# State space convolution: bias and last tap moved from TensorE to GpSimd and VectorE

## The chip, the cores and the metric

The kernel runs on all 8 cores of one Trainium2 chip, one batch element to a core, with the same program and no exchange between cores. The metric is the device time in microseconds of the slowest core.

## The reference, cut to what matters

Two layers of a hybrid decoder. Each layer adds to x (8 x 2048 x 1024, float32) the output projection of four mixers that share one normalised input projection, and then a SwiGLU. One of the mixers is a state space scan, whose input first goes through a causal convolution of four taps along the sequence, each of 768 channels by itself, with a bias and a silu:

```python
SSM_CONV_K = 4
SSM_CONV_DIM = SSM_D_INNER + 2 * SSM_GROUPS * SSM_D_STATE   # 768
...
def ssd_mixer(h, conv_w, conv_b, dt_bias, a_log, d_skip, norm_w):
    z, xbc, dt = jnp.split(h, [SSM_D_INNER, SSM_D_INNER + SSM_CONV_DIM], axis=-1)
    xbc = lax.conv_general_dilated(
        xbc, conv_w.T[:, None, :], window_strides=(1,), padding=[(SSM_CONV_K - 1, 0)],
        dimension_numbers=('NWC', 'WIO', 'NWC'), feature_group_count=SSM_CONV_DIM)
    xbc = jax.nn.silu(xbc + conv_b)
    xs, Bm, Cm = jnp.split(xbc, [SSM_D_INNER, SSM_D_INNER + SSM_GROUPS * SSM_D_STATE], axis=-1)
```

The other mixers are a gated MLP over chunks of 128 positions, a pooling over windows of 2 to 16 positions, and a differential attention.

## The kernel before, in words

Activations lie transposed, channels on the 128 partitions and positions along the free dimension, in slabs of 512 positions. The sequence of 2048 is worked in two halves `h` of two slabs `s` each. The outer loops are: layer `li`, half `h`, and in them `mixing(li, h)` followed by `swiglu(li, h)`.

In `mixing`, the state space part runs for each slab over six blocks `cb` of 128 channels. `b1_proj` projects a block with eight matmuls; ScalarE copies the result as bf16 into `cin[cb % 2]`, behind three carried columns that GpSimd copies in and out of `carry`. `b1_conv` then makes the convolution on TensorE: one matmul with 12 rows adds the bias (`cvb` holds it as a high and a low bf16 part, six rows each, and the moving operand is one constant column repeated 512 times), and four matmuls with the diagonal matrices `dws[:, cb, kk, :]` add the taps, each reading `cin` shifted by one position. `silu2` closes: tanh on ScalarE, reading PSUM, then one `scalar_tensor_tensor` on VectorE, whose second input is the PSUM bank. The results are scaled by two, as the tanh form of silu leaves them. After the six blocks `b2_chunk` runs the scan, four chunks of 128 positions a slab, and `ssd_norm` its norm. The attention and the output projection with the second norm follow.

`layer_params` loads each layer's parameters once, builds the 24 diagonal matrices with VectorE, and makes the two-part biases with `hilo`. The gating bias `gbs` of the first mixer is such a one too, of 8 rows.

The order of all instructions on all five queues is not that of the text. `Prog.schedule` takes the atoms (a matmul group between `begin` and `end`, or one instruction), their dependencies and a modelled duration for each, and puts them in order greedily: the earliest possible start first, ties by priority. `mixing` has a high priority (`P.bias = 2000`), `swiglu` the lowest (`P.bias = None`), so that the SwiGLU of one half fills TensorE's gaps in the mixing of the next. PSUM banks are given out by the same planner. In `mixing(0, 0)` there is nothing yet to fill with.

The calls of a slab:

```python
            for cb in range(6):
                if cb + 1 < 6:
                    b1_proj(s, cb + 1)
                b1_conv(s, cb)
            for c in range(4 * s, 4 * s + 4):
                b2_chunk(c)
```

Of the kernel before, what the change touches and what calls it, by code (L numbers as in the profile page):

```python
# [8 lines left out]
F32 = mybir.dt.float32  # L9
BF16 = mybir.dt.bfloat16  # L10
# [571 lines left out]
GELU_C = 0.7978845608028654  # L582


CP_N1W, CP_N2W, CP_CONVW, CP_DCOL, CP_SSMNW, CP_PSCALE, CP_QNW, CP_KNW, CP_SUBLN = 0, 8, 16, 40, 42, 44, 46, 47, 48
NCOLP = 49

RP_GMNW, RP_DTB, RP_ALOG, RP_LQ1, RP_LK1, RP_LQ2, RP_LK2 = 0, 256, 260, 264, 296, 328, 360
NROWP = 392

CF_U, CF_SL, CF_ALIBI, CF_INVWIN, CF_INVC16, CF_M6, CF_M4 = 0, 128, 256, 324, 326, 358, 360
NCF = 362
CB_IDENT, CB_U, CB_NEG, CB_BD32, CB_BD64, CB_HEAD, CB_CB, CB_SEL = 0, 128, 256, 384, 512, 640, 644, 650
NCB = 682


def make_consts():
    cf = np.zeros((128, NCF), np.float32)
    cb = np.zeros((128, NCB), np.float32)
    j = np.arange(128)[:, None]  # L600
    l = np.arange(128)[None, :]
    cf[:, CF_U:CF_U + 128] = (j <= l)
    cf[:, CF_SL:CF_SL + 128] = (j > l)
    for h in range(4):
        for e in range(17):
            cf[:, CF_ALIBI + h * 17 + e] = SLOPES[h] * (np.arange(128) - 128.0 * e)
# [6 lines left out]
    cf[0:6, CF_M6] = 1.0
    cf[6:12, CF_M6 + 1] = 1.0
    cf[0:4, CF_M4] = 1.0
    cf[4:8, CF_M4 + 1] = 1.0
    cb[:, CB_IDENT:CB_IDENT + 128] = np.eye(128)
    cb[:, CB_U:CB_U + 128] = (j <= l)
    cb[:, CB_NEG:CB_NEG + 128] = np.where(j <= l, 0.0, NEGV)
    cb[:, CB_BD32:CB_BD32 + 128] = (j // 32 == l // 32)  # L620
    cb[:, CB_BD64:CB_BD64 + 128] = (j // 64 == l // 64)
    for p in range(8):
        cb[p, CB_HEAD + p % 4] = 1.0
    for p in range(12):
        cb[p, CB_CB + p % 6] = 1.0
    for p in range(96):
        cb[p, CB_SEL + p % 32] = 1.0
    return cf, cb
# [31 lines left out]
def build(nlayers=2):  # L660
# [10 lines left out]
    wd_d = din("ffn_w_down", [2, DFF, D])  # L671
    wsT_d = din("gm_wsT", [2, 4, 128, 128])
    gbs_d = din("gm_bs", [2, 4, 128])
    cvb_d = din("ssm_conv_b", [2, 6, 128])
    poolw_d = din("pool_w", [2, 4, 64, 64])
    colp_d = din("colp", [2, 128, NCOLP])
    rowp_d = din("rowp", [2, 1, NROWP])
# [35 lines left out]
    colp = sb("colp", [128, NCOLP], F32)  # L713
    rowp = sb("rowp", [128, NROWP], F32)
    small = sb("small", [128, 32], F32)
    cvb = sb("cvb", [12, 128], BF16)
    gbs = sb("gbs", [8, 128], BF16)
    wsTm = sb("wsTm", [128, 4, 128], BF16)
    wdt = sb("wdt", [128, 8, 4], BF16)
    dtp = sb("dtp", [128, 6, 32], F32)  # L720
    atm3 = tp[:, 1024:1024 + 384].bitcast(F32)
    R3 = sb("R3", [128, 128], BF16)
    hist = sb("hist", [128, 2, 16], F32)
    carry = sb("carry", [128, 6, 4], BF16)
    wbd = sb("wbd", [128, 2, 128], BF16)
    dws = sb("dws", [128, 6, 4, 128], BF16)
    Sst = sb("Sst", [128, 256], F32)
    Sbf = sb("Sbf", [128, 256], BF16)
    Psum.ap = es.enter_context(nc.psum_tensor(PSUM_NAME, [128, 8, 512], F32))
# [2 lines left out]
    Ub = cB[:, CB_U:CB_U + 128]  # L732
    NEGb = cB[:, CB_NEG:CB_NEG + 128]
    bd32b = cB[:, CB_BD32:CB_BD32 + 128]
    bd64b = cB[:, CB_BD64:CB_BD64 + 128]
    Uf = cF[:, CF_U:CF_U + 128]
    SLf = cF[:, CF_SL:CF_SL + 128]
    neghalf = small[:, 31:32]
# [59 lines left out]
    def layer_params(li, pbuf, pbase):  # L798

        lam_init = 0.8 - 0.6 * math.exp(-0.3 * li)  # L800
        load_w(wsTm[:], wsT_d[li].rearrange("h s t -> s h t"), 'wsT')
        for cc in range(2):
            P.memset('pool', wbd[:, cc, :], 0.0)
            for gg in range(2):
                load_w(wbd[gg * 64:(gg + 1) * 64, cc, gg * 64:(gg + 1) * 64], poolw_d[li][2 * cc + gg], 'wbd')
        tb = Bump(pbuf, pbase, pbase + 6 * KB)
        cf2 = tb.alloc([128], F32)[0:12]
        ch2 = tb.alloc([128], BF16)[0:12]
        for r in range(2):
            P.dma('sp', cf2[6 * r:6 * r + 6], cvb_d[li], 'cvb', wrs=[cf2[6 * r:6 * r + 6]], kb=6)  # L810
        hilo(cvb[:], cf2, ch2, cF[0:12, CF_M6:CF_M6 + 1], cF[0:12, CF_M6 + 1:CF_M6 + 2])
        gf2 = tb.alloc([128], F32)[0:8]
        gh2 = tb.alloc([128], BF16)[0:8]
        lt = tb.alloc([32], F32)
        for r in range(2):
            P.dma('sp', gf2[4 * r:4 * r + 4], gbs_d[li], 'gbs', wrs=[gf2[4 * r:4 * r + 4]], kb=2)
        P.ts('dve', gf2, gf2, 0.5, None, op0=ALU.mult)
        hilo(gbs[:], gf2, gh2, cF[0:8, CF_M4:CF_M4 + 1], cF[0:8, CF_M4 + 1:CF_M4 + 2])
        P.stt(wsTm[:], wsTm[:], 0.5, Ub.unsqueeze(1).to_broadcast([128, 4, 128]), ALU.mult, ALU.mult)
        for k, (ra, rb) in enumerate(((RP_LQ1, RP_LK1), (RP_LQ2, RP_LK2))):  # L820
            P.tt('dve', lt, rowp[:, ra:ra + 32], rowp[:, rb:rb + 32], ALU.mult)
            P.rsum(lam2[:, k:k + 1], lt)
        P.act(lam2, lam2, AF.Exp)
        P.tt('dve', neglam, lam2[:, 1:2], lam2[:, 0:1], ALU.subtract)
        P.ts('dve', neglam, neglam, -lam_init, None, op0=ALU.add)
        P.ts('dve', qnws, colp[:, CP_QNW:CP_QNW + 1], SM_SCALE, None, op0=ALU.mult)
        P.ts('dve', subc, colp[:, CP_SUBLN:CP_SUBLN + 1], 1.0 - lam_init, None, op0=ALU.mult)
        P.ts('dve', dcol, colp[:, CP_DCOL:CP_DCOL + 2], 0.5, None, op0=ALU.mult)
        P.act(Ab, rowp[:, RP_ALOG:RP_ALOG + 4], AF.Exp)
        P.ts('dve', Ab, Ab, -1.0, None, op0=ALU.mult)  # L830
        for cb in range(6):
            for kk in range(4):
                cw = CP_CONVW + cb * 4 + kk
                P.ts('dve', dws[:, cb, kk, :], identb, colp[:, cw:cw + 1], None, op0=ALU.mult)
        P.memset('dve', carry[:], 0.0)
        P.memset('dve', hist[:], 0.0)
        P.memset('dve', Sst[:], 0.0)
        P.memset('dve', Sbf[:], 0.0)

    def mixing(li, h):  # L840
# [87 lines left out]
        for t in range(8):  # L928
# [124 lines left out]
        def b2_chunk(c):
            s, cl = c // 4, slice((c % 4) * 128, (c % 4) * 128 + 128)
# [282 lines left out]
def host_pack(inputs):  # L1337
# [4 lines left out]
    for l in range(2):  # L1342
        colp[l, :, CP_N1W:CP_N1W + 8] = f('norm1_w')[l].reshape(8, 128).T
        colp[l, :, CP_N2W:CP_N2W + 8] = f('norm2_w')[l].reshape(8, 128).T
        colp[l, :, CP_CONVW:CP_CONVW + 24] = f('ssm_conv_w')[l].reshape(6, 128, 4).transpose(1, 0, 2).reshape(128, 24)
        for hc in range(2):
            colp[l, :, CP_DCOL + hc] = f('ssm_d')[l][2 * hc + p // 64]
        colp[l, :, CP_SSMNW:CP_SSMNW + 2] = f('ssm_norm_w')[l].reshape(2, 128).T
        colp[l, :, CP_PSCALE:CP_PSCALE + 2] = f('pool_scale')[l].reshape(2, 128).T
        colp[l, :, CP_QNW] = f('da_q_norm_w')[l][p % 32]  # L1350
        colp[l, :, CP_KNW] = f('da_k_norm_w')[l][p % 32]
        colp[l, :, CP_SUBLN] = f('da_subln_w')[l][p % 64]
        rowp[l, 0, RP_GMNW:RP_GMNW + 256] = f('gm_norm_w')[l].reshape(256)
# [41 lines left out]
```

How the kernel before makes its waits and increments, by code:

```python
        def run(engname, e):  # L472
            for waits, thunk, tok in plan[engname]:
                alone = list(waits) if thunk is None else list(waits[:-1])
                for k in range(0, len(alone), 2):
                    w_ins = e.wait_ge(semh[alone[k][0]], alone[k][1])
                    if k + 1 < len(alone):
                        w_ins._wait_ge(semh[alone[k + 1][0]], alone[k + 1][1])
                if thunk is None:
                    continue
                ins = thunk(e)
                if waits:
                    s, v = waits[-1]
                    ins._wait_ge(semh[s], v)
                ins.then_inc(semh[tok[0]], 16 if tok[0].startswith('d_') else 1)
```

## Time and profile before

| | |
|---|---|
| median of 3 runs | 1833.38 us (1832.42 to 1893.77) |
| the profiled execution | 1833.44 us |
| its span on the slowest core | 1831.9 us (cores 1822.4 to 1831.9) |
| TensorE busy | 1723.5 us, 94% |
| VectorE busy | 1033.6 us, 56% |
| ScalarE busy | 802.4 us, 44% |
| GpSimd busy | 505.4 us, 28% |
| mean granted TensorE clock, core 0 | 0.966 of full |

Busy time is the union of an engine's instructions over the span of the slowest core. Matmuls overlap, so the duration of one is longer than the distance between two starts.

### The profile page before, as it was taken

To read this page: it belongs to the slowest core of one execution; us is meant where nothing else is said; L and a number is where in the kernel's file an instruction comes from. 1 tells how busy PE (TensorE), PEld (TensorE's weight loads), DVE (VectorE), ACT (ScalarE), POOL (GpSimd) and SP (SyncE) were. 2 spreads that over 40 slices of the span, in tenths; PEclk is the share of its full clock that TensorE was granted. 3 is DMA by queue.
4 is the path that set the end of the run, shared out by engine and by line. 5 is a ranking of instruction groups with operands and counts; after the bars stand their busy time and mean duration, and the time that the engine had idled before them with its cause. 6 is when DMAs were issued, how large, how long until landed. Compare 5 with 4: busy or idle time off the path is not lost.

```text
span 1831.9 us, 25845 instructions; the slowest of 8 cores (1822.4 to 1831.9 us)
## 1 busy us (share of the span) xinstructions
PE 1723.5 (94%) x10492; PEld 793.1 (43%) x10492; DVE 1033.6 (56%) x1947; ACT 802.4 (44%) x1218; POOL 505.4 (28%) x659
## 2 busy tenths in 40 slices
PE   3998789999999999999999988999999999999998
PEld 0444334444444444544444443444444444444443
DVE  2766547767533458668655456666664333655555
ACT  1477633446576723213455553225466674211110
POOL 4345444633121121024332232033431111100000
PEclk9997589999999999999999999999999999999999
DMA  9303944324630249752145246930517202684433
GB/s 181 43 24 67 199 94 56 52 29 60 124 64 7 45 83 150 148 75 43 30 63 97 42 89 123 164 51 1 92 24 138 42 6 58 110 162 74 70 46 104
DMA packets 123464, 143.38 MB, mean 78 GB/s; under 512 B 9128, under 2 KB 91600, under 8 KB 123344
## 3 DMA queue, kind: packets, MB, share of 16 engines
q0 software_dynamic: 100912, 99.11, 36.7%
q1 hardware_dynamic: 22432, 42.61, 7.1%
q8 instruction: 83, 1.36, 0.3%
q14 instruction: 37, 0.30, 0.1%
HBM read 224.03 MB, written 16.78 MB: 131 GB/s over the span
## 4 chain that ended last, share of the span: by engine, by line
PE 85%; DVE 6%; ACT 5%; DMA 2%; POOL 2%; issue 0%; SPq 0%; DVEq 0%; ACTq 0%
PE ps L513 84%; DVE s_hT L551 2%; DMA s_x<-xT 1%; ACT s_x L532 1%; PE ps L517 1%; ACT s_tmp L532 1%; ACT s_pt L532 1%; DVE s_x L541 1%; ACT L532 1%; POOL s_mix L541 1%; POOL s_x L541 0%; DVE s_ring L551 0%; DVE s_ring L541 0%; DMA s_x<-xspill 0%; DVE s_sg L551 0%
## 5 line engine op out<-in xcount | busy, mean ns | idle before, releaser
L513 PE MATMUL ps<-s_hT,s_ring 128*128 128x512 bf16 x2816 | 665.3, 383 | 5.4 <-DVE s_hT L551 4.0
L541 DVE TENSOR_TENSOR s_x<-s_x,ps 128x512 f32<-128x512 f32 (+2 forms) x496 | 317.7, 671 | 195.4 <-PE ps L513 184.4
L513 PEld LDWEIGHTS ps<-s_hT,s_ring 128*128 128x128 bf16 x2816 | 265.4, 98 | 308.8 <-issue 20.6
L513 PE MATMUL ps<-s_act,s_ring 128*128 128x512 bf16 x1408 | 343.6, 385 | 15.6 <-DVE s_sg L551 9.7
L532 ACT ACTIVATE s_sg<-ps 128x512 f32<-128x512 f32 x176 | 104.7, 597 | 420.3 <-PE ps L513 419.7
L551 DVE SCALAR_TENSOR_TENSOR s_sg<-s_sg,ps 128x512 f32<-128x512 f32 x176 | 119.8, 685 | 241.4 <-ACT s_sg L532 135.9
L541 POOL TENSOR_TENSOR s_x<-s_x 128x512 bf16<-128x512 f32 (+2 forms) x116 | 111.9, 965 | 332.4 <-DVE s_x L541 218.4
L513 PEld LDWEIGHTS ps<-s_act,s_ring 128*128 128x128 bf16 x1408 | 131.1, 99 | 164.9 <-issue 12.7
L513 PE MATMUL ps<-s_hT,s_x 128*128 128x512 bf16 x768 | 181.8, 387 | 1.3 <-DVE s_hT L551 1.0
L551 DVE SCALAR_TENSOR_TENSOR s_act<-s_sg,ps 128x512 bf16<-128x512 f32 x176 | 119.7, 685 | 72.0 <-PE ps L513 70.5
L513 PE MATMUL ps<-s_x,s_k 32*128 32x512 bf16 (+3 forms) x668 | 115.7, 344 | 8.8 <-ACT s_act L532 1.8
L532 ACT ACTIVATE s_pt<-ps,s_cF 128x1024 bf16<-128x1024 f32 (+3 forms) x109 | 97.1, 890 | 47.2 <-PE ps L513 46.9
L513 PEld LDWEIGHTS ps<-s_hT,s_x 128*128 128x128 bf16 x768 | 75.4, 99 | 94.6 <-DVE s_hT L551 5.3
L216 POOL DMA_DIRECT2D s_ring<-ffn_w_down x24 | 18.9, 788 | 318.1 <-PE ps L513 317.3
L532 ACT ACTIVATE s_tmp<-ps,s_cF 128x1024 bf16<-128x1024 f32 (+3 forms) x92 | 84.8, 923 | 45.1 <-PE ps L513 44.3
L532 ACT ACTIVATE s_x<-ps,s_cF 128x1024 bf16<-128x1024 f32 (+3 forms) x92 | 82.5, 897 | 39.2 <-PE ps L513 38.0
L513 PE MATMUL ps<-s_mix,s_hT 128*128 128x260 bf16 (+1 forms) x512 | 91.5, 327 | 2.9 <-DVE s_x L541 2.9
L541 POOL TENSOR_TENSOR s_mix<-s_x 128x512 bf16<-128x512 f32 x48 | 54.3, 1137 | 137.3 <-PE ps L513 120.9
L532 ACT ACTIVATE s_x<-ps 128x512 f32<-128x512 f32 x84 | 49.8, 596 | 86.5 <-PE ps L513 62.5
L532 ACT ACT_TABLE_LOAD x64 | 82.1, 1283 | 2.8 <-PEq L661 1.1
L513 PEld LDWEIGHTS ps<-s_x,s_k 32*128 32x128 bf16 x668 | 31.5, 91 | 104.0 <-issue 49.6
L551 DVE SCALAR_TENSOR_TENSOR s_hT<-s_x,s_colp,s_tmp 128x512 bf16<-128x512 f32 x64 | 45.2, 768 | 45.1 <-ACT s_tmp L532 45.1
(196 smaller groups left out, 2028.1 us busy)
## 6 DMA issues: line engine op xcount, KB each, us to landing
s_ring<-ffn_w_gate POOLq DMA_DIRECT2D x20, 1024.0 KB, 13.3
s_ring<-ffn_w_up POOLq DMA_DIRECT2D x20, 1024.0 KB, 11.8
s_ring<-ffn_w_down POOLq DMA_DIRECT2D x20, 1024.0 KB, 10.1
s_x<-w_in POOLq DMA_DIRECT2D x12, 1024.0 KB, 24.6
s_x<-xT SPq DMA_DIRECT2D x16, 512.0 KB, 5.9
s_x<-xT SPq DMA_DIRECT2D x8, 1024.0 KB, 11.7
xspill<-s_x SPq DMA_DIRECT2D x8, 1024.0 KB, 13.9
s_x<-xspill SPq DMA_DIRECT2D x8, 1024.0 KB, 8.4
```

What stands on the lines that cost most here:

```text
L216: self.add(Op(queue, lambda e: e.dma_start(out=out, in_=in_), list(rds), list(wrs), dur, None, 'd_' + key, kb))
L513: self.op('pe', lambda e: e.matmul(real(out), lhsT, rhs, start=start, stop=stop), [lhsT, rhs], [out], d if dur is None else dur)
L517: self.op('pe', lambda e: e.transpose(real(out), in_, ident), [in_, ident], [out], 0.06)
L532: self.op('act', lambda e: e.activation(out, real(in_), func, **kw), rd, [out], d, self.TAB.get(func))
L541: self.op(eng, lambda e: e.tensor_tensor(out, real(in0), real(in1), op), [in0, in1], [out], d)
L551: self.op('dve', lambda e: e.scalar_tensor_tensor(out, real(in0), scalar, real(in1), op0, op1), [in0, scalar, in1], [out], 0.06 + self.vdu ...
```

## The change

The bias and the last tap are computed together by one GpSimd `tensor_scalar` per block: `u = ci[:, 3:515] * w3 + bias`, from bf16 to float32, with both scalars taken from per-partition columns of `colp`. TensorE does only the taps 0 to 2 and no bias. VectorE adds the PSUM bank to `u` in place, and `silu2` reads `u` from SBUF, with ScalarE and with VectorE. `uu` holds two such buffers. The constants for the bias (`cvb`, its selector columns and masks, its DMAs and its `hilo`) go, as do six of the 24 diagonal matrices of a layer. `gbs` moves from partitions 0 to 7 of a buffer of its own to partitions 96 to 103 of `R3`, and unused constants go.

```diff
+    uu = sb("uu", [128, 2, 512], F32)
...
-    cvb = sb("cvb", [12, 128], BF16)
-    gbs = sb("gbs", [8, 128], BF16)
...
+    gbs = R3[96:104, :]
...
-    dws = sb("dws", [128, 6, 4, 128], BF16)
+    dws = sb("dws", [128, 6, 3, 128], BF16)
...
-        cf2 = tb.alloc([128], F32)[0:12]
-        ch2 = tb.alloc([128], BF16)[0:12]
-        for r in range(2):
-            P.dma('sp', cf2[6 * r:6 * r + 6], cvb_d[li], 'cvb', wrs=[cf2[6 * r:6 * r + 6]], kb=6)
-        hilo(cvb[:], cf2, ch2, cF[0:12, CF_M6:CF_M6 + 1], cF[0:12, CF_M6 + 1:CF_M6 + 2])
-        gf2 = tb.alloc([128], F32)[0:8]
-        gh2 = tb.alloc([128], BF16)[0:8]
+        gf2 = tb.alloc([128], F32)[96:104]
+        gh2 = tb.alloc([128], BF16)[96:104]
...
         for cb in range(6):
-            for kk in range(4):
+            for kk in range(3):
                 cw = CP_CONVW + cb * 4 + kk
                 P.ts('dve', dws[:, cb, kk, :], identb, colp[:, cw:cw + 1], None, op0=ALU.mult)
...
-            P.mm(pg[:, 0:256], gbs[:], cB[0:8, CB_HEAD:CB_HEAD + 4].unsqueeze(2).to_broadcast([8, 4, 64]), start=True, stop=False)
+            P.mm(pg[:, 0:256], gbs, cB[96:104, CB_HEAD:CB_HEAD + 4].unsqueeze(2).to_broadcast([8, 4, 64]), start=True, stop=False)
...
+        us = [uu[:, k, :] for k in range(2)]
...
         def b1_conv(s, cb):
             ci = cin[cb % 2]
             dst = slabs[s % len(slabs)][1 + cb // 2][:, cb % 2, :]
+            u = us[cb % len(us)]
+            cw = CP_CONVW + cb * 4 + 3
+            P.ts('pool', u, ci[:, 3:515], colp[:, cw:cw + 1], colp[:, CP_CONVB + cb:CP_CONVB + cb + 1], op0=ALU.mult, op1=ALU.add)
             b = P.tile(m1)
             P.begin()
             P.guards = [dst]
-            P.mm(b, cvb[:], cB[0:12, CB_CB + cb:CB_CB + cb + 1].to_broadcast([12, 512]), start=True, stop=False)
-            for kk in range(4):
-                P.mm(b, dws[:, cb, kk, :], ci[:, kk:kk + 512], start=False, stop=(kk == 3))
+            for kk in range(3):
+                P.mm(b, dws[:, cb, kk, :], ci[:, kk:kk + 512], start=(kk == 0), stop=(kk == 2))
             P.end()
-            silu2(dst, b)
+            P.tt('dve', u, u, b, ALU.add)
+            silu2(dst, u)
```

## Rows read from the trace of the kernel before

**Rows 1.** The page's busy time by engine: us, share of the span, instructions.

```profile
PE 1723.5 (94%) x10492; PEld 793.1 (43%) x10492; DVE 1033.6 (56%) x1947; ACT 802.4 (44%) x1218; POOL 505.4 (28%) x659
```

**Rows 2.** The page's 40 slices: TensorE busy and granted clock, in tenths.

```profile
PE   3998789999999999999999988999999999999998
...
PEclk9997589999999999999999999999999999999999
```

**Rows 3.** Windows on core 0: length, busy time by engine, granted clock, DMA share, GB/s.

```profile
60.00:110.00 50.00, 47.45 (x254) 23.26 (x253) 31.04 (x88) 25.81 (x45) 20.19 (x36) 0.97 0.01 2
110.00:170.00 60.00, 54.84 (x417) 26.13 (x416) 40.19 (x88) 43.08 (x74) 34.31 (x48) 0.83 0.22 53
170.00:230.00 60.00, 44.10 (x383) 22.91 (x383) 34.22 (x72) 40.56 (x67) 29.39 (x31) 0.63 0.91 170
...
340.00:450.00 110.00, 109.90 (x658) 51.47 (x655) 72.40 (x167) 55.97 (x105) 47.52 (x79) 1.00 0.25 37
...
830.00:960.00 130.00, 129.99 (x756) 60.05 (x754) 89.53 (x186) 59.61 (x112) 54.70 (x89) 1.00 0.25 40
...
1230.00:1330.00 100.00, 98.82 (x587) 46.60 (x587) 66.64 (x148) 46.57 (x89) 42.66 (x73) 1.00 0.27 43
```

**Rows 4.** Timeline of TensorE around two convolutions, 402 to 415 us: start, length, what.

```profile
401.96 7.07 PE L513 MATMUL ps<-s_hT,s_x 128*128 128x512 bf16 x32
...
408.96 0.39 PE L513 MATMUL ps<-s_cB,s_cvb 12*128 12x512 bf16 x1
409.28 1.04 PE L513 MATMUL ps<-s_wx,s_dws 128*128 128x512 bf16 x4
...
410.25 0.38 PE L513 MATMUL ps<-s_cB,s_cvb 12*128 12x512 bf16 x1
...
410.57 1.04 PE L513 MATMUL ps<-s_wx,s_dws 128*128 128x512 bf16 x4
...
411.44 3.62 PE L513 MATMUL ps<-s_hT,s_x 128*128 128x512 bf16 x16
```

**Rows 5.** Groups by shape, whole span: busy us, mean ns; idle before and releasers.

```profile
L541 DVE TENSOR_TENSOR s_x<-s_x,ps 128x512 f32<-128x512 f32 x448 | 292.3, 684 | 181.4 <-PE ps L513 173.0 <-DMA s_x<-xspill 6.3
...
L541 POOL TENSOR_TENSOR s_x<-s_x 128x512 bf16<-128x512 f32 x56 | 64.4, 1151 | 67.3 <-DVE s_x L558 37.5 <-PE ps L513 15.3 <-DVE s_x L551 10.4
...
L532 ACT ACTIVATE s_x<-s_x 128x512 f32<-128x512 f32 x68 | 42.5, 628 | 5.4 <-DVE s_x L551 5.2
...
L551 DVE SCALAR_TENSOR_TENSOR s_hT<-s_x,s_colp,s_mix 128x512 bf16<-128x512 f32 x64 | 44.7, 768 | 9.0 <-ACT s_mix L532 9.0
...
L551 DVE SCALAR_TENSOR_TENSOR s_x<-s_wx,ps 128x512 bf16<-128x512 f32 x48 | 32.1, 685 | 51.1 <-PE ps L513 36.6 <-ACT s_wx L532 14.3
...
L532 ACT ACTIVATE s_wx<-ps 128x512 f32<-128x512 f32 x48 | 27.6, 596 | 30.7 <-PE ps L513 19.5 <-DVE s_x L551 11.2
...
L541 POOL TENSOR_TENSOR s_ring<-s_ring,s_x 128x512 bf16<-128x512 f32 x8 | 10.6, 1321 | 4.9 <-ACT s_ring L532 4.9
L558 POOL COPY s_wx<-s_carry 128x3 bf16<-128x3 bf16 x36 | 7.7, 217 | 22.9 <-PE ps L513 22.9
...
L547 DVE TENSOR_SCALAR s_dws<-s_cB,s_colp 128x128 bf16<-128x128 bf16 x48 | 8.5, 254 | 0.8 <-DMA s_colp<-colp 0.7
```

**Rows 6.** The chain that ended last, first half: start, us, what, instructions.

```profile
71.40 10.78 PE ps L513 x51
...
103.14 9.99 PE ps L513 x46
...
128.06 12.11 PE ps L513 x75
...
164.09 1.37 PE ps L513 x5
```

**Rows 7.** The same chain where one half hands over to the next.

```profile
256.23 7.03 POOL s_mix L541 x7
...
1135.42 7.36 DVE s_hT L551 x12
```

More of the change, by code:

```diff
@@ L582 @@
 GELU_C = 0.7978845608028654
-CP_N1W, CP_N2W, CP_CONVW, CP_DCOL, CP_SSMNW, CP_PSCALE, CP_QNW, CP_KNW, CP_SUBLN = 0, 8, 16, 40, 42, 44, 46, 47, 48
-NCOLP = 49
+CP_N1W, CP_N2W, CP_CONVW, CP_DCOL, CP_SSMNW, CP_PSCALE, CP_QNW, CP_KNW, CP_SUBLN, CP_CONVB = 0, 8, 16, 40, 42, 44, 46, 47, 48, 49
+NCOLP = 55
 RP_GMNW, RP_DTB, RP_ALOG, RP_LQ1, RP_LK1, RP_LQ2, RP_LK2 = 0, 256, 260, 264, 296, 328, 360
 NROWP = 392
[L591 to L594, printed above, removed]
+CF_U, CF_SL, CF_ALIBI, CF_INVWIN, CF_INVC16, CF_M4 = 0, 128, 256, 324, 326, 358
+NCF = 360
+CB_IDENT, CB_U, CB_NEG, CB_BD32, CB_HEAD, CB_SEL = 0, 128, 256, 384, 512, 516
+NCB = 548
 def make_consts():
@@ L612, in make_consts @@
                 cf[p, CF_INVC16 + c * 16 + t] = 1.0 / min(t + 1, win)
[L613 to L616, printed above, removed]
+    cf[96:100, CF_M4] = 1.0
+    cf[100:104, CF_M4 + 1] = 1.0
     cb[:, CB_IDENT:CB_IDENT + 128] = np.eye(128)
@@ L620, in make_consts @@
     cb[:, CB_BD32:CB_BD32 + 128] = (j // 32 == l // 32)
-    cb[:, CB_BD64:CB_BD64 + 128] = (j // 64 == l // 64)
     for p in range(8):
-        cb[p, CB_HEAD + p % 4] = 1.0
-    for p in range(12):
-        cb[p, CB_CB + p % 6] = 1.0
+        cb[96 + p, CB_HEAD + p % 4] = 1.0
     for p in range(96):
@@ L673, in build @@
     gbs_d = din("gm_bs", [2, 4, 128])
-    cvb_d = din("ssm_conv_b", [2, 6, 128])
     poolw_d = din("pool_w", [2, 4, 64, 64])
@@ L715, in build @@
     small = sb("small", [128, 32], F32)
-    cvb = sb("cvb", [12, 128], BF16)
-    gbs = sb("gbs", [8, 128], BF16)
     wsTm = sb("wsTm", [128, 4, 128], BF16)
-    wdt = sb("wdt", [128, 8, 4], BF16)
     dtp = sb("dtp", [128, 6, 32], F32)
@@ L734, in build @@
     bd32b = cB[:, CB_BD32:CB_BD32 + 128]
-    bd64b = cB[:, CB_BD64:CB_BD64 + 128]
     Uf = cF[:, CF_U:CF_U + 128]
@@ L817, in layer_params @@
         P.ts('dve', gf2, gf2, 0.5, None, op0=ALU.mult)
-        hilo(gbs[:], gf2, gh2, cF[0:8, CF_M4:CF_M4 + 1], cF[0:8, CF_M4 + 1:CF_M4 + 2])
+        hilo(gbs, gf2, gh2, cF[96:104, CF_M4:CF_M4 + 1], cF[96:104, CF_M4 + 1:CF_M4 + 2])
         P.stt(wsTm[:], wsTm[:], 0.5, Ub.unsqueeze(1).to_broadcast([128, 4, 128]), ALU.mult, ALU.mult)
@@ L1345, in host_pack @@
         colp[l, :, CP_CONVW:CP_CONVW + 24] = f('ssm_conv_w')[l].reshape(6, 128, 4).transpose(1, 0, 2).reshape(128, 24)
+        colp[l, :, CP_CONVB:CP_CONVB + 6] = f('ssm_conv_b')[l].reshape(6, 128).T
         for hc in range(2):
@@ L1368, in host_pack @@
         "gm_bs": np.ascontiguousarray(f('gm_bs')),
-        "ssm_conv_b": np.ascontiguousarray(f('ssm_conv_b').reshape(2, 6, 128)),
         "pool_w": np.ascontiguousarray(f('pool_w')),
```

## The prediction

> **What bounds the kernel now.** I read the page's busy line first: TensorE is busy 1723.5 of 1831.9 us, 94%, against 56% for VectorE, 44% for ScalarE and 28% for GpSimd [rows 1]. The 40 slices of 45.8 us then say where the missing 6% is: the first slice (input and first norm, 3 tenths), slices 4 to 6 (8, 7 and 8 tenths), and specks later; the granted clock is 7, 5 and 8 tenths in slices 4 to 6 and about full after [rows 2]. The reader should see two kernels in one: the first half of layer 0 (to about 230 us), with no SwiGLU to fill in, and the rest, where it fills.
>
> The windows make it plain [rows 3]. The three later stretches with the convolutions, 340 to 450, 830 to 960 and 1230 to 1330 us, hold 48 tap matmuls each (12 convolutions), and TensorE is busy 109.9 of 110, 130.0 of 130 and 98.8 of 100 us at granted clock 1.00. There time is TensorE work and nothing else. The first half holds the other 12 convolutions: TensorE is busy 102.3 of 110 us between 60 and 170, then only 44 of 60, with the clock at 0.83 and 0.63.
>
> **What a convolution costs TensorE.** The timeline of a stretch without a stall gives start-to-start times [rows 4]. An ordinary 512-column matmul takes (3.62 - 0.38) / 15 = 0.216 us. The one of 12 rows starts 408.96 - (401.96 + 7.07 - 0.38) = 0.31 us after its predecessor, and the first tap starts 0.32 us after it; four taps to the next projection are 411.44 - 410.57 = 0.87, four ordinary steps. So the bias matmul is dearer than its 512 columns: 0.10 us extra on entering it and 0.10 on leaving it. Before: 0.10 + 0.32 + 4 x 0.216 = 1.28 us. After: 3 x 0.216 = 0.65. Saved: 0.63 us for each of the 48 convolutions (6 blocks x 2 slabs x 2 halves x 2 layers), 30.2 us of TensorE work.
>
> The Trainium skill, "TensorE: Matmul & The Clock Gate", section "Why this matters for your kernels", says that a matmul of few rows takes the same time as one of 128. By that the saving would be 96 x 0.216 = 20.7 us. The trace disagrees at the seams. "TensorEngine Tiling (Array Packing)", section "Key Properties", says that a change of tiling mode drains the array; the two seams of 0.10 us fit that. I go by the rows.
>
> **The covered convolutions.** 36 x 0.63 = 22.7 us leave stretches in which TensorE has 1.3 us of idle time in 340 [rows 3]. Nothing has to be made up elsewhere: the SwiGLU atoms fill in whatever waits. I count all 22.7.
>
> **What is added.** VectorE: 48 additions, one input in PSUM, at 0.684 us (the same form stands in the profile), and the closing scalar_tensor_tensor reads both tensors from SBUF: 0.768 us in the nearest row against 0.685 now [rows 5]. That is 48 x (0.684 + 0.083) = 36.8 us; 12 of the 48 diagonal builds go (12 x 0.254 = 3.0) and eight small operations for the bias. In 340 to 450 VectorE goes from 72.4 by 12 x 0.77 = 9.2 to 82 of 110 us: hidden. Cost nothing there; without TensorE as cover it would be 9.2 us a half. ScalarE: tanh from SBUF instead of PSUM, 0.628 against 0.596, 1.5 us in all, hidden.
>
> GpSimd: 48 tensor_scalar with two per-partition scalars, 128x512, bf16 to f32. No such form is in the trace. From below: the 3-column copy, 0.217 us. From above: the slowest tensor_tensor form of this size, 1.321. The commonest is 1.151; I take 1.1, since width and conversion are the same and one input fewer can only help [rows 5]. In 340 to 450 GpSimd goes from 47.5 to 61 of 110 us; even at 1.321 to 63. The Trainium skill, "GPSIMD Engine Reference", section "Engine selection", would put elementwise work on VectorE: GpSimd about twice slower with two inputs, roughly level with one. No run here shows the one-input case; by it the instruction would be near 0.7 us and my total about 2 us lower.
>
> **The waits it adds.** The addition waits for three taps and for GpSimd. Behind it on VectorE stand evictions of SwiGLU and of the state space chunks, and behind those TensorE's PSUM banks. The tensor_scalar waits for ScalarE's copy of the projection, and behind it on GpSimd stand the carry copies, for which the next convolution's matmuls wait, and the issues of ring weights. One convolution's time from copy to silu: before 1.18 us of matmuls; after 1.1 + 0.68, and 0.08 + 0.03 in the silu, with one more handover: longer by about 0.8 to 0.9 us. In the covered halves two `cin` buffers and the fill hide that: a block's eleven matmuls take 2.4 us, above GpSimd's 1.1 and VectorE's 1.5.
>
> **The first half.** There 12 x 0.63 = 7.5 us of TensorE work goes, in a stretch (60 to 170 us) where TensorE is 93% busy. Against it stands the longer way. The chain runs through TensorE blocks that hold convolutions at 71, 103, 128 and 164 us, with a fifth pair inside the first [rows 6]: five times 0.9 = 4.5 us. I book 7.5 - 4.5 = 3.0 us of gain, with bounds of -5 (all twelve pay the 0.9, 10.8 us, and VectorE's 9.2 us press on it, little of the saving arrives) and +7.5 (no latency shows). From 170 to 205 the chain is VectorE and GpSimd work of the chunks, which the change doesn't touch. The other edits (dropped constants, four small SP transfers, the gating bias now in rows 96 to 103 of `R3`, still one narrow matmul) I put at zero: the transfers ran beside the input norm.
>
> **The sum.** 22.7 + 3.0 = 25.7 us. The profiled execution took 1833.44 us with a span of 1831.9, and the median is 1833.38, so they are the same time: 1833.4 - 25.7 = 1807.7, forecast 1808, 1.4% faster. What is late next is still TensorE: its work falls to about 1693 us. A measurement of this kernel tells about 2% from no change, so I expect "within 2%".
>
> **Rivals.**
> A. The seams stay: they belong to the start of an accumulation group and not to the 12 rows. For: both are at a group's start. Against: projections start groups without one, 411.44 being an example. Then 20.7 - 5.2 = 15.5 us covered, and 5.2 - 4.5 = 0.7: 1833.4 - 16.2 = 1817. Chance 0.10.
> B. The planner's order. `schedule` is greedy and rebuilds the order of 25,000 instructions; TensorE's idle time (1831.9 - 1723.5 = 108 us, almost all outside the covered convolutions) isn't fixed. The hand-overs are the fragile places: 7.0 us of GpSimd squares at 256 us and 7.4 us of VectorE at 1135 us stand alone on the chain [rows 7]. If such a place opens twice more, 14 us go: 1808 + 14 = 1822. Chance 0.18.
> C. Slower: GpSimd paces the first half. If each tensor_scalar queues behind another operation of its size (1.151), the way per convolution grows by 2.0 us, 12 x 2.0 = 24, less the 7.5 saved: 16.5 us. TensorE then idles more between 60 and 130, where the clock was 0.97, and falls to 1.2 GHz, as it did to 0.63 in the stretch with 44 of 60 us busy: 60 us of work at 0.63 in place of 0.97 cost 60 x (0.97/0.63 - 1) = 32 us. 1833.4 - 22.7 + 16.5 + 32 = 1859. It decides for slower once the first half loses over 22.7 us. Against: GpSimd is busy 20 of 50 and 34 of 60 us there. Chance 0.04.
> D. All 30.2 us arrive, no latency shows, and the first half keeps the clock better. A mean of 0.63 over 60 us [rows 3] is some 44 us at 1.2 GHz and the rest at 2.4; if 16 of the 44 us went at 2.4, their work would take 8: 1833.4 - 30.2 - 8 = 1795. Chance 0.13. The one-input GpSimd would push this way.
>
> **How the numbers follow.** Forecast (1801 to 1816 by its own bounds) 0.55, A 0.10, B 0.18, C 0.04, D 0.13. Low end: between forecast and D, 1797, leaving 0.09 below. High end: B with 7 us more, 1829, leaving 0.07 above. Faster by over 2% (under 1796.7): most of D, 0.09. Slower by over 2% (over 1870): the far part of C, 0.01. The rest, 0.90, is the same.
>
> **What the profile after would show.** No matmul of 12 rows; 144 tap matmuls; TensorE's start-to-start 0.22 us into and through the taps; three stretches with convolutions still 99% busy and 7.5 us shorter each; VectorE about 1067 us, GpSimd about 558. A tensor_scalar of 1.1 us. Wrong would be: TensorE idle before the addition's release in covered stretches, convolution pairs in the first half spread further apart, or work gone but idle grown by as much (B).

## The result, and the profile after

The changed kernel takes 1803.9 us (1801.9 to 1804.0) against 1833.4: a ratio of 0.9838, 95% interval 0.981 to 0.9867. Timed again beside its own variants it gave 0.9837 (0.9822 to 0.9853). That is 29.5 us or 1.6% less, and clear of the noise; I had forecast 25.7 us, and that a measurement could hardly tell it from no change. Runs in which one die was disturbed, in either kernel, are left out of every ratio here.

The page of the profiled execution (1801.94 us, its slowest core 1800.4), against [rows 1, 2]:

```profile
span 1800.4 us, 25725 instructions; the slowest of 8 cores (1788.1 to 1800.4 us)
## 1 busy us (share of the span) xinstructions
PE 1693.7 (94%) x10396; PEld 789.6 (44%) x10396; DVE 1059.5 (59%) x1975; ACT 813.9 (45%) x1226; POOL 542.5 (30%) x707
...
PE   3996888999999999999999999999999999999998
...
PEclk9996698999999999999999999999999999999999
```

TensorE lost 29.8 us of busy time and 96 matmuls; what is left over, 1800.4 - 1693.7 = 106.7 us of idle, was 1831.9 - 1723.5 = 108.4. So the first reading is simple: the work went, the idle time stayed about what it was. GpSimd gained 37 us where I had 53, VectorE 26 where I had 34.

Windows, answering to [rows 3] (the first three at the same times, the others around the later convolutions, which start earlier now; core 1):

```profile
60.00:110.00 50.00, 46.30 (x256) 23.13 (x254) 36.62 (x88) 28.68 (x50) 27.59 (x44) 0.97 0.06 18
110.00:170.00 60.00, 48.95 (x367) 25.33 (x365) 53.90 (x121) 44.03 (x79) 50.36 (x64) 0.83 0.35 78
170.00:230.00 60.00, 49.20 (x444) 25.68 (x444) 23.81 (x49) 41.27 (x61) 20.09 (x21) 0.63 0.79 137
...
350.00:430.00 80.00, 77.59 (x442) 37.29 (x441) 57.71 (x125) 39.37 (x72) 39.75 (x70) 0.98 0.21 32
845.00:920.00 75.00, 75.00 (x438) 35.69 (x438) 56.14 (x109) 35.77 (x67) 37.33 (x65) 1.00 0.11 15
1210.00:1285.00 75.00, 75.00 (x437) 35.59 (x436) 53.95 (x108) 37.43 (x68) 36.44 (x66) 1.00 0.27 43
```

Two of the three later stretches are full to the last digit. The first of them is not: it has 2.4 us of idle in 80, and in the wider window of [rows 3], 340 to 450 us, TensorE is busy 106.6 of 110 us (105.6 on core 0), where it was 109.9. Only 0.3 us of it is a wait for the new addition. The rest waits for results of ScalarE and VectorE that the change does not touch:

```profile
PE ps L513 <- ACT s_mix L556: 0.9, 1, 0.9
PE ps L513 <- ACT s_mix L532: 0.8, 1, 0.8
PE ps L513 <- DVE s_sg L551: 0.7, 1, 0.7
...
PE ps L513 <- DVE s_uu L541: 0.3, 1, 0.3
```

The first half looks different from before: between 110 and 170 us VectorE is busy 53.9 of 60 (40.2 before) and GpSimd 50.4 (34.3), and after 170 both are light. The planner has written another order: the last tap matmul of the first half starts at 147.9 us, before at 165.1.

TensorE around a convolution, against [rows 4]:

```profile
407.66 3.63 PE L513 MATMUL ps<-s_hT,s_x 128*128 128x512 bf16 x16 [0.35 <-DVE s_uu L541]
411.12 0.81 PE L513 MATMUL ps<-s_wx,s_dws 128*128 128x512 bf16 x3
411.77 3.62 PE L513 MATMUL ps<-s_hT,s_x 128*128 128x512 bf16 x16
```

Last projection matmul at 407.66 + 3.63 - 0.38 = 410.91, first tap at 411.12, next projection at 411.77: 0.21 us in, 0.65 for the three taps. The seams are gone. The first line also shows the new wait, 0.35 us for VectorE's addition: it is there, and rare (over the whole span TensorE waits for the buffer `uu` four times, 3.2 us in all).

What the new instructions cost, by the tile `uu` (duration ns: least, median, most):

```profile
L541 DVE TENSOR_TENSOR s_uu<-s_uu,ps x48: 670/686/689, 74.5 to 1285.8; 128x512 f32<-128x512 f32 x48
L547 POOL TENSOR_SCALAR s_uu<-s_wx,s_colp x36: 757/768/1307, 360.5 to 1284.6; 128x512 f32<-128x512 bf16 x36
...
L551 DVE SCALAR_TENSOR_TENSOR s_x<-s_wx,s_uu x36: 681/685/1528, 373.1 to 1289.9; 128x512 bf16<-128x512 f32 x36
```

GpSimd's instruction takes 0.77 us in the median, not 1.1; single ones take up to 1.67, and the mean is 0.84. The closing operation with both tensors in SBUF has the median that it had with one in PSUM, 0.685; single ones take up to 1.53 us, the means of the two groups are 0.73 and 0.82, and nothing here shows what lengthens them.

### The profile page after: what moved, and what is told of

Read it like the earlier page. It is cut to its first block, busy times and chain, and to the rows that moved or that the text cites. A ratio compares the mean times of both kernels' runs of the same rounds, so it can differ in the third digit from the quotient of the medians.

```text
span 1800.4 us, 25725 instructions; the slowest of 8 cores (1788.1 to 1800.4 us)
## 1 busy us (share of the span) xinstructions
PE 1693.7 (94%) x10396; PEld 789.6 (44%) x10396; DVE 1059.5 (59%) x1975; ACT 813.9 (45%) x1226; POOL 542.5 (30%) x707
## 4 chain that ended last, share of the span: by engine, by line
PE 87%; DVE 5%; ACT 4%; DMA 2%; POOL 1%; issue 1%; SPq 0%; DVEq 0%; ACTq 0%; POOLq 0%
PE ps L513 86%; DVE s_hT L551 2%; DMA s_x<-xT 2%; ACT s_x L532 1%; PE ps L517 1%; DVE s_x L541 1%; ACT s_tmp L532 1%; DVE s_ring L541 1%; ACT L532 1%; ACT s_pt L532 0%; DVE s_x L551 0%; DVE s_sg L551 0%; ACT s_act L532 0%; POOL s_x L541 0%; SPq L216 0%
## 5 line engine op out<-in xcount | busy, mean ns | idle before, releaser
L216 POOL DMA_DIRECT2D s_ring<-ffn_w_down x24 | 18.9, 787 | 300.9 <-PE ps L513 295.8
L513 PE MATMUL ps<-s_mix,s_hT 128*128 128x260 bf16 (+1 forms) x512 | 96.7, 337 | 4.1 <-DVE s_hT L551 2.7
L541 POOL TENSOR_TENSOR s_mix<-s_x 128x512 bf16<-128x512 f32 x48 | 50.4, 1052 | 105.4 <-PE ps L513 88.9
L532 ACT ACTIVATE s_x<-ps 128x512 f32<-128x512 f32 x72 | 42.5, 596 | 84.7 <-PE ps L513 51.6
L513 PEld LDWEIGHTS ps<-s_mix,s_hT 128*128 128x128 bf16 x512 | 49.6, 100 | 44.5 <-DVE s_hT L551 4.9
## 6 DMA issues: line engine op xcount, KB each, us to landing
s_ring<-ffn_w_up POOLq DMA_DIRECT2D x20, 1024.0 KB, 11.1
s_x<-xT SPq DMA_DIRECT2D x8, 1024.0 KB, 10.4
```

The lines of the kernel that those rows point to most:

```text
L216: self.add(Op(queue, lambda e: e.dma_start(out=out, in_=in_), list(rds), list(wrs), dur, None, 'd_' + key, kb))
L513: self.op('pe', lambda e: e.matmul(real(out), lhsT, rhs, start=start, stop=stop), [lhsT, rhs], [out], d if dur is None else dur)
L532: self.op('act', lambda e: e.activation(out, real(in_), func, **kw), rd, [out], d, self.TAB.get(func))
L541: self.op(eng, lambda e: e.tensor_tensor(out, real(in0), real(in1), op), [in0, in1], [out], d)
```

## The experiments

Each ratio is against the kernel before, on the same chip; 0.001 is 1.8 us. Many of them hold the order of instructions: the planner is told that an added operation lasts nothing, or that a removed one is still there, so that the queues differ by that operation alone. Where that was not done, the instruction and the order changed together, and with the order the PSUM banks that the planner gives out.

**The bias matmul over 128 rows.**

```diff
-            P.mm(b, cvb[:], cB[0:12, ...].to_broadcast([12, 512]), start=True, stop=False)
+            P.mm(b, cvb[:], cB[:, ...].to_broadcast([128, 512]), start=True, stop=False)
```

> The kernel before, with its bias matmul widened from 12 to 128 rows (rows 12 to 127 are zeros), so the same 512 columns and the same result, only the row count differs. My theory (the 0.10 us seams into and out of the matmul belong to its 12 rows): every convolution loses 0.20 us of TensorE time, 48 x 0.20 = 9.6 us, start-to-start 0.22 us through the whole convolution, TensorE busy about 1714 us, time about 1824, ratio 0.995. Rival A (the seams belong to the start of an accumulation group): start-to-start stays 0.31 and 0.32 us, time unchanged at 1833. A rival by the new order of the planner doesn't apply: the modelled durations are the same, so the order is.

Ratio 0.9926 (0.9909 to 0.9942), 13.6 us less (10.6 to 16.7). The order was the same on all five engines; VectorE has two more instructions, which set the rows to zero. TensorE's timeline:

```profile
407.34 0.38 PE L513 MATMUL ps<-s_cB,s_cvb 128*128 128x512 bf16 x1
407.56 1.03 PE L513 MATMUL ps<-s_wx,s_dws 128*128 128x512 bf16 x4
408.42 0.38 PE L513 MATMUL ps<-s_cB,s_cvb 128*128 128x512 bf16 x1
408.64 1.03 PE L513 MATMUL ps<-s_wx,s_dws 128*128 128x512 bf16 x4
```

0.22 us out of the bias matmul and (408.42 - 407.56) / 4 = 0.215 into it, where [rows 4] have 0.32 and 0.31. The seams belong to the 12 rows; rival A falls. More rows of zeros make this kernel faster. The 4 us beyond the 9.6 are not the seams' work. The mean granted clock of the cores was 0.9715 in these executions against 0.9686 in the kernel before, 0.003 of the span; my estimate from that is 5 us less time lost to the lower clock. What raised the clock is not shown.

**The bias matmul left out.**

```diff
-            P.mm(b, cvb[:], cB[0:12, ...].to_broadcast([12, 512]), start=True, stop=False)
```

> The kernel before without the bias matmul: the bias is left out, four taps stay on TensorE, nothing is added elsewhere. Theory of the seams: 48 x (0.63 - 0.216) = 19.9 us of TensorE time go, time about 1813, ratio 0.989. Rule that few rows cost what 128 do: 48 x 0.216 = 10.4 us, time about 1823. If the order rebuilt by the planner matters more than either, the time falls outside 1808 to 1828.

Ratio 0.9861 (0.9847 to 0.9876), 25.5 us less, more than either theory's number. The planner's order differed here, so this mixes the 19.9 us with an order and decides nothing between them.

**A fourth tap back on TensorE.**

```diff
-            for kk in range(3):
-                P.mm(b, dws[:, cb, kk, :], ci[:, kk:kk + 512], start=(kk == 0), stop=(kk == 2))
+            for kk in range(4):
+                P.mm(b, dws[:, cb, kk % 3, :], ci[:, kk:kk + 512], start=(kk == 0), stop=(kk == 3))
```

> The changed kernel with a fourth tap matmul put back on TensorE beside the GpSimd instruction (it uses the first tap's weights again, so the fourth tap is counted twice, once wrongly). It prices one 128-row matmul of 512 columns per convolution with all else kept. Theory (TensorE work is time in every stretch, the first half too): 48 x 0.216 = 10.4 us more than the changed kernel's 1804, so 1814, ratio 0.9895. Rival (in the first half other engines set the pace): 36 x 0.216 = 7.8 us, 1812, and the first half's end does not move.

Ratio 0.9813 (0.9799 to 0.9828): more TensorE work and 4 us faster than the changed kernel. A miss for both theories, though the intervals of the two kernels just touch (0.9822 is the low end of the changed one). The planner's order was the suspect, so I held the order:

```diff
+                     ..., dur=0.0 if kk == 3 else None)
```

> The changed kernel with the fourth tap matmul put back beside the GpSimd instruction (first tap's weights again, so that tap is counted wrongly), and with the changed kernel's order held: the planner counts the extra matmul as zero. Theory (the earlier run without the extra time was the planner's new order, which saved what the matmuls cost): 48 x 0.216 = 10.4 us over the changed kernel, about 1813, TensorE idle as in the changed kernel. Rival (a tap is free beside the GpSimd path): 1801 to 1805.

Ratio 0.9856 (0.984 to 0.9872). The same instructions as the run before in another order: 0.0043 or 7.9 us apart, with intervals that do not touch. That is rival B at work, and it can help as well as hurt. But a tap now seemed to cost 3 us, not 10.4, so it was run again beside the changed kernel.

> The changed kernel once more, timed beside its fixed-order variants. 0.9838 again if the first ratio was right, 1802 to 1804 us; the other three are read against this one.

0.9837 (0.9822 to 0.9853).

> The fourth tap matmul put back in the changed kernel's order (first tap's weights again), repeated. Theory (TensorE work is time everywhere): 10.4 us over the changed kernel of the same chip. Rival (8 us or less, the later halves only): 7.8 us. If it is under 4 us, TensorE work is not all of the time.

0.9851 (0.9836 to 0.9867), 2.6 us more than the changed kernel. The spans by core tell part of why. The changed kernel (first profile), then this one:

```profile
core 0: 1788.6 us, clock 0.974
core 1: 1800.4 us, clock 0.965
core 2: 1789.9 us, clock 0.973
core 3: 1799.9 us, clock 0.963
core 4: 1799.5 us, clock 0.967
core 5: 1789.7 us, clock 0.972
core 6: 1792.3 us, clock 0.970
core 7: 1788.1 us, clock 0.971
```

```profile
core 0: 1806.0 us, clock 0.972
core 1: 1800.8 us, clock 0.971
core 2: 1801.0 us, clock 0.971
core 3: 1804.6 us, clock 0.971
core 4: 1806.7 us, clock 0.969
...
core 6: 1800.2 us, clock 0.973
```

With the extra tap every core has about the same clock and ends within 7 us. In this execution the changed kernel falls into two sets: five cores at 1788 to 1792 us, three at 1800; their mean clocks are 0.970 to 0.974 and 0.963 to 0.967. In its other executions the cores lie anywhere between 1788 and 1806 us. The metric takes the slowest. Between single cores of like clock (0.971 and 0.970 against 0.971) the tap costs 1800.8 - 1788.1 to 1792.3, 9 to 13 us, around the 10.4. Windows of the changed kernel on core 0, then core 1, show where the sets part:

```profile
320.00:360.00 40.00, 35.80 (x208) 18.45 (x211) 33.52 (x79) 17.17 (x33) 27.10 (x43) 1.00 0.17 28
530.00:550.00 20.00, 18.70 (x182) 9.02 (x184) 8.01 (x13) 16.60 (x21) 0.73 (x1) 1.00 0.01 2
625.00:655.00 30.00, 28.76 (x251) 13.38 (x255) 13.55 (x24) 19.37 (x22) 4.72 (x5) 1.00 0.11 36
```

```profile
320.00:360.00 40.00, 36.34 (x196) 18.75 (x195) 30.30 (x68) 16.11 (x32) 19.56 (x29) 0.91 0.28 45
530.00:550.00 20.00, 18.95 (x191) 9.03 (x189) 4.74 (x9) 15.86 (x18) 4.43 (x4) 0.91 0.00 1
625.00:655.00 30.00, 28.47 (x252) 12.29 (x252) 9.19 (x16) 22.20 (x23) 1.47 (x2) 0.89 0.08 10
```

Core 1 is granted 1.2 GHz for part of three stretches in which core 0 keeps 2.4, though TensorE is 90 to 96% busy in them on both. With the extra tap, core 1 keeps 1.00 at 530 and at 625.

But the slowest core is not the whole of it. On the mean of the eight cores, over all executions on that chip, the tap costs 1801.7 - 1796.3 = 5.4 us, not 10.4. The next table splits the mean span of one profile of each kernel. "Idle" is TensorE's idle time. "Slowed" is my estimate of the time lost to the lower clock: busy time x (1 - granted clock), summed over windows of 20 us. What remains is TensorE's work at full speed. Work and slowed time are good to about 3 us: the same matmuls come out as 1640.9, 1642.6 and 1643.7 us of work in three kernels.

| kernel, mean of 8 cores, us | span | work | idle to 280 us | slowed to 280 us | idle after | slowed after |
|---|---|---|---|---|---|---|
| before | 1826.9 | 1670.6 | 65.2 | 25.9 | 47.1 | 18.1 |
| changed (`after_again`) | 1797.3 | 1640.9 | 65.9 | 26.5 | 45.1 | 18.9 |
| fourth tap, held order (`a_tap_fixed2`) | 1803.1 | 1651.3 | 65.2 | 24.9 | 46.0 | 15.7 |
| fourth tap, free order (`a_tap_back`) | 1795.9 | 1651.9 | 68.5 | 32.8 | 35.7 | 7.0 |
| GpSimd twice, held order (`a_ts_fixed2`) | 1795.6 | 1643.7 | 66.7 | 24.0 | 48.6 | 12.6 |
| bare saving, old order (`b_3taps_fixed2`) | 1801.2 | 1642.6 | 67.3 | 27.4 | 48.1 | 15.8 |

The tap adds 1651.3 - 1640.9 = 10.4 us of work, the idle time stays (111.2 against 111.0), and 4.8 us less go to the lower clock (2.8 in the profiles of the first pair). So a matmul's work arrives in full as work, and the clock gives part of it back, on the mean core too. Against the held order, the free order of the same matmuls has 11 us more idle and slowed time up to 280 us, and 19 us less after.

**GpSimd's instruction twice**, free order and then held order.

```diff
             P.ts('pool', u, ci[:, 3:515], colp[:, cw:cw + 1], ...)
+            P.ts('pool', u, ci[:, 3:515], colp[:, cw:cw + 1], ...)
```

> The changed kernel with its GpSimd instruction issued twice per convolution (same inputs, same output), which makes the side path 0.77 us longer before VectorE's addition. Theory (the side path is hidden everywhere): time unchanged within 4 us of 1804, GpSimd busy up by 37 us. Rival (the prediction's step: each convolution of the first half pays its longer way): 5 to 12 times 0.77, 4 to 9 us more, and the first half ends that much later. Rival C (GpSimd paces): more than 15 us.

Ratio 0.9872 (0.9856 to 0.9889), 6 us more than the changed kernel. By itself it would have confirmed the wrong theory (the side path is felt).

> The changed kernel with the GpSimd instruction issued twice, order held: the planner counts the second as zero. Theory (hidden; the 8 us of the earlier run were the new order): within 3 us of the changed kernel's 1804. Rival (the side path ends last in the first half): 4 to 9 us more, and TensorE idle before the first SwiGLU up by as much.

Ratio 0.9825 (0.9811 to 0.9839).

> GpSimd's instruction twice, in the changed kernel's order, repeated. Theory (side path hidden): within 2 us of the changed kernel. Rival (first half pays): 4 to 9 us more.

Ratio 0.9834 (0.9816 to 0.9852), against 0.9837 of the changed kernel on that chip. GpSimd is busy 579.0 us in place of 542.5, its results come 0.77 us later, and the time does not show it. In the table TensorE's idle time up to 280 us is 66.7 us against 65.9, where twelve waits of 0.77 us would have made it 9.2 us more. So the side path is hidden in the first half. Later there are 3.5 us more of idle, and 6.3 us less of slowed time go with them. The 6 us were the order that a longer modelled duration called for: same instructions, 0.9872 against 0.9825.

**The bare saving in the old order.**

```diff
-            P.mm(b, cvb[:], cB[0:12, ...].to_broadcast([12, 512]), start=True, stop=False)
-            for kk in range(4):
-                P.mm(b, dws[:, cb, kk, :], ci[:, kk:kk + 512], start=False, stop=(kk == 3))
+            for kk in range(3):
+                P.mm(b, dws[:, cb, kk, :], ci[:, kk:kk + 512], start=(kk == 0), stop=(kk == 2), dur=...)
```

> The kernel before with neither the bias matmul nor the last tap (both are left out and nothing takes their place), and its order of instructions held on every engine: the planner is told the old duration and the old dependencies. So this is the TensorE saving of the change alone, 48 x 0.63 = 30.2 us, in the old order. Theory (TensorE's work is the time, in the first half too): 1833.4 - 30.2 = 1803, ratio 0.984, the same as the changed kernel. Rival (in the first half others set the pace): 22.7 to 25 us, time 1809 to 1811, ratio 0.987. If it is faster than the changed kernel by more than 5 us, the added work and waits cost that.

Ratio 0.9854 (0.984 to 0.9868).

> The kernel before without bias matmul and last tap (both left out), in the old order, repeated. If the added work and waits cost nothing and the new order is worth nothing, it equals the changed kernel within 2 us. If the new order is the better one, it is 3 to 6 us slower; if the additions cost, it is faster.

Ratio 0.9869 (0.9851 to 0.9886). So 24 to 27 us come from TensorE's 30.2 us of work alone. That is no matter of the slowest core: on the mean of the eight cores it is 25.6 us on this chip and 26.8 on the one of the first ratio. In the table 2.1 us more idle and 1.5 us more slowed time than before stand against it up to 280 us, so in the first half some 2 to 4 of its 7.5 us seem not to arrive. The changed kernel, with all its additions, is faster than this by 0.0032 or 6 us on the same chip (by 3 us from the first ratios). The two intervals touch, but the mean of the eight cores settles that there is a difference: 1795.1 to 1797.3 us in the executions of the changed kernel, 1801.2 to 1801.8 in those of the bare saving, 5.2 us. In the table the difference is idle time, 111.0 us against 115.4, and added work doesn't take idle time away. The dropped constants could a little, and were not tested apart; up to 110 us TensorE is idle 35.2 us in the bare saving and 34.9 in the changed kernel, so not at the start of layer 0. What is left is the new order. TensorE's first matmul of SwiGLU moves with it, on core 7 of before, of the bare saving and of the changed kernel:

```profile
L513 PE MATMUL ps<-s_hT,s_ring x2816: 376/379/634, 269.3 to 1817.2; 128*128 128x512 bf16 x188
```

```profile
L513 PE MATMUL ps<-s_hT,s_ring x2816: 376/379/634, 264.7 to 1789.4; 128*128 128x512 bf16 x188
```

```profile
L513 PE MATMUL ps<-s_hT,s_ring x2816: 377/379/634, 255.4 to 1778.6; 128*128 128x512 bf16 x188
```

The saving alone moves that start by 4.6 us, the new order by another 9.3 (2.9 to 4.1 and 7.8 to 8.2 on the mean of the cores). But it doesn't tell how much is won: the free order of `a_tap_back` has this start at 271.6 us on the mean core, the changed kernel at 257.5, and ends no later. Of the 4.4 us less of idle time only 1.4 lie before 280 us, and 3.0 after.

**The planner told 0.77 us.**

```diff
-                self.vdur(eng, width(out)))
+                0.19 + width(out) * 0.00113 if eng == 'pool' else self.vdur(eng, width(out)))
```

> The changed kernel, same instructions, but the planner is told 0.77 us for GpSimd's tensor_scalar of 512 columns in place of 1.175. Nothing but the order changes. It measures what the order alone is worth: theory: TensorE busy unchanged within 3 us, idle time moves by up to 8 us to either side, time 1796 to 1812. Rival (order is worth nothing): within 2 us of 1804. A correct duration need not give the better order.

Ratio 0.9851 (0.9832 to 0.987), 2.4 us above the changed kernel: inside the uncertainty. The true duration gave no better order.

**The tensor_scalar on VectorE.**

```diff
-            P.ts('pool', u, ...)
+            P.ts('dve', u, ...)
```

> The changed kernel with its tensor_scalar on VectorE in place of GpSimd; everything else the same. It says whether the choice of GpSimd matters. TensorE work unchanged. On VectorE the instruction (one input, SBUF) should take 0.3 to 0.6 us, 48 x 0.5 = 24 us at most. Theory (hidden in the three later halves, felt in the first, where VectorE is 54 of 60 us busy between 110 and 170): 2 to 6 us over the changed kernel, 1806 to 1810. Rival (VectorE has room everywhere): 1804, or less, since one handover between engines goes.

Ratio 0.9883 (0.9868 to 0.9897), 8 us more than the changed kernel. It takes 0.54 us there and ends a handover, and still it loses: the windows of its slowest core have 41.8 of 60 us of TensorE between 110 and 170, at a clock of 0.76, and 0.53 in the next 60 us. This kernel ran in an order of its own, and an order was worth 8 us above. So that GpSimd is the better place because it is the idle engine is likely from the windows, and not shown.

**Toward a faster kernel.** Two edits, each alone and together: one more tap off TensorE, on VectorE, and the gating bias over 128 rows.

```diff
-            for kk in range(3):
+            for kk in range(2):
...
+            P.stt(u, ci[:, 2:514], colp[:, cw - 1:cw], u, ALU.mult, ALU.add)
             P.tt('dve', u, u, b, ALU.add)
```

> The changed kernel with one more tap taken off TensorE: VectorE adds tap 2 to u by one scalar_tensor_tensor of 512 columns before it adds the PSUM bank, TensorE keeps taps 0 and 1. Theory (VectorE hidden while it is under 90% busy where TensorE is full): 48 x 0.216 = 10.4 us less TensorE work against about 48 x 0.75 = 36 us more VectorE, time about 1794, ratio 0.978. Rival (VectorE, 54 of 60 us busy between 110 and 170 in the changed kernel, becomes the pace of the first half): 12 x 0.75 = 9 us lost there, so 1800 to 1803, the same as the changed kernel, with TensorE idle up by about 8.

Ratio 0.9841 (0.9828 to 0.9854): 10.4 us of TensorE work went and nothing came of it. The first half of that kernel, the same windows as above:

```profile
110.00:170.00 60.00, 42.61 (x296) 21.60 (x294) 54.63 (x122) 43.43 (x81) 39.87 (x50) 0.85 0.40 80
170.00:230.00 60.00, 51.10 (x463) 28.43 (x464) 25.57 (x54) 43.17 (x60) 33.85 (x37) 0.50 0.49 97
```

VectorE 54.6 of 60 us, TensorE down to 42.6, then 1.2 GHz for the whole of the next 60 us. TensorE's waits for VectorE's additions into `ring` between 110 and 170 us (us in total, times, longest), in this kernel and in the changed one:

```profile
PE ps L513 <- DVE s_ring L541: 7.1, 4, 4.4
```

```profile
PE ps L513 <- DVE s_ring L541: 1.5, 2, 1.0
```

Of TensorE's 17.4 us of idle there 11.8 end with a result of VectorE; in the changed kernel it is 3.4 of 11.1. So VectorE sets the pace here, in this kernel's own order; with the order held it was not tried.

```diff
-            P.mm(pg[:, 0:256], gbs, cB[96:104, ...].to_broadcast([8, 4, 64]), start=True, stop=False)
+            P.mm(pg[:, 0:256], R3[:], cB[:, ...].to_broadcast([128, 4, 64]), start=True, stop=False)
```

> The changed kernel with the gating bias matmul (8 rows, 256 columns, 32 of them) widened to 128 rows: the whole of R3 as weights against a constant that is zero outside rows 96 to 103. Same result. The seam theory, on another matmul: start-to-start from it to the next falls from 0.21 to 0.11 us and the step into it by 0.10, 32 x 0.20 = 6.4 us less TensorE work, time 1797 to 1799, ratio 0.980, less or more by up to 6 us since the planner's order changes with one new dependency. Rival (seams only hurt 512-column matmuls): TensorE busy unchanged, time 1804.

The seam went, as with the other bias. The changed kernel, then this one:

```profile
344.83 2.75 PE L513 MATMUL ps<-s_act,s_ring 128*128 128x512 bf16 x12
347.51 0.28 PE L513 MATMUL ps<-s_cB,s_R 8*128 8x256 bf16 x1
347.72 0.29 PE L513 MATMUL ps<-s_x,s_wsTm 128*128 128x64 bf16 x4
```

```profile
340.62 4.05 PE L513 MATMUL ps<-s_hT,s_ring 128*128 128x512 bf16 x18
344.50 0.27 PE L513 MATMUL ps<-s_cB,s_R 128*128 128x256 bf16 x1
344.61 0.28 PE L513 MATMUL ps<-s_x,s_wsTm 128*128 128x64 bf16 x4
```

In: 347.51 - (344.83 + 2.75 - 0.38) = 0.31 against 0.21. Out: 0.21 against 0.11. By 32 such matmuls that is 6.4 us of work (an estimate from this one place). The time is inconclusive: 0.9887 (0.9833 to 0.994), and the order had changed.

> Both edits together: two taps on TensorE and the gating bias over 128 rows. If both theories hold, 16.8 us less TensorE work than the changed kernel, time about 1787, ratio 0.974. If VectorE paces the first half, 1794 to 1797.

Ratio 0.9929 (0.9889 to 0.9968). It has less TensorE work than any other kernel here, by the matmuls taken out, and it is slower than the changed one: its lowest time is 1807.4 us. Again the order was its own.

## Where the prediction held, and which step failed

**TensorE's work.** Right: 0.63 us per convolution, 30.2 us in all; TensorE's busy time fell by 29.8, its work at full speed by 29.7 in the table. The seams that I read from start-to-start times are real and belong to the few rows, shown by the 128-row version of each bias. The rule that few rows cost what 128 do, by which the saving would have been 20.7 us, doesn't hold at the seams.

**The covered convolutions.** Right: with the order held, idle and slowed time after 280 us are 63.9 us in the bare saving and 65.2 before, so as far as the table can tell all 22.7 us arrived. "Still 99% busy" failed in one of the three stretches, 340 to 450 us, which has 97%; its new idle time is almost all in places that the change doesn't touch, so it came with the order.

**The first half.** This is the step that failed: "five times 0.9 = 4.5 us" for the longer way of a convolution. The longer way cost nothing that the runs can show: with everything that was added, the changed kernel is faster than the bare saving. (VectorE's addition was not tested by itself.) GpSimd's instruction was bounded rightly (0.217 to 1.321) and taken wrongly: 0.77, not 1.1; the row I leaned on had two inputs. The Trainium skill, "GPSIMD Engine Reference", section "Engine selection", has GpSimd roughly level with VectorE on one input; my estimate from that, 0.7, was near. The runs agree with the rule only in part: the same instruction takes 0.54 us on VectorE. Lengthening the way by a further 0.77 us cost nothing measurable with the order held (0.9825 and 0.9834 against 0.9838 and 0.9837). My argument took the old chain and put the new durations on it, but the chain belonged to the old order. In its place the runs showed two things that the sum did not have. In the old order, with nothing added at all, 3 to 6 us of TensorE's 30.2 do not arrive. And the new order, which the forecast put at nothing and rival B at a loss, is 3 to 6 us faster than the old.

**The sum.** 25.7 us forecast, 29.5 measured. The difference is about the 4.5 us that I booked against the change. The nearness of both numbers is luck: the saving alone gave 24 to 27 us, which is my 25.7 without the reason that I gave for it, and the new order gave about as much again as was missing from 30.2. The last step of the sum was wrong too: "about 2% from no change". The interval is 0.3% to either side, and 1.6% stands far outside it.

**The rivals.** A fell. B, the order, is real at the size given, about 8 us, twice shown with the same instructions (0.9813 against 0.9856; 0.9872 against 0.9825), but here it fell on the good side. C needed GpSimd to pace the first half; doubling its instruction did nothing to the time. D had the right work and the wrong clock: between 170 and 230 us it was 0.63 in the windows of before (core 0) and after (core 1), and 0.67 and 0.68 on the mean of the eight cores.

**VectorE as cover.** I wrote that its extra work costs nothing where TensorE is full, and that held. In the first half the changed kernel stands near the edge: with more on VectorE, in `a_2taps` and with the tensor_scalar there, the kernels came out no faster or slower, each in an order of its own.

Still open: what raised the clock with the 128-row bias, what in the new order is the better part, and what makes one core drop to 1.2 GHz where another with the same program keeps 2.4.

## What to carry to other kernels

Where TensorE is the bound, read its work from start-to-start times and not from counts of columns: a matmul of few rows between full ones costs a seam on each side. Padding it with zero rows gained 13.6 us on the kernel before, without another engine; on the second such matmul the seam went too, but the time didn't show it. Where a planner writes the order, an experiment that adds or removes an operation also draws a new order, worth as much here as the effect looked for; tell the planner that nothing changed, and only then read the difference. Read it on all cores, since the slowest one alone gave 2.6 us where their mean gave 5.4. Work moved off a bound engine goes to the one with room in the stretch with least cover, and there a second helping may cost what the first one gained.

## What the runs showed of the hardware

A matmul of 12 rows and 512 columns among ones of 128 rows: 0.31 us from its predecessor's start and 0.32 to its successor's, where 128 rows have 0.215 to 0.22. One of 8 rows and 256 columns: 0.31 and 0.21, with 128 rows 0.21 and 0.11. GpSimd's tensor_scalar with two per-partition scalars, 512 columns, bf16 to float32: 0.77 us in the median (mean 0.84), against a mean of 1.15 for its two-input tensor_tensor; on VectorE the same instruction takes 0.54. Eight cores with one program and their own data do not share a clock history: in one execution they ended 12 us apart, and with one more matmul in each convolution within 7 us of each other.
